# An expert stage on one core: the wait of v's rounding, and the place of the gathered rows' additions

## The chip, the cores and the metric

The kernel runs on one core of a Trainium2 chip. The metric is the device time of one execution in microseconds (us). All of the change lies in one of its stages, the one that computes the experts of a PEER layer (product-key retrieval). That stage takes about 2390 of 5121 us.

## The reference, cut to what matters

The whole program is one layer of an encoder: token mixers, cross-attention and then PEER. Of PEER, for 1152 tokens (1024 of a prompt, 128 of samples), this counts here:

```
idx = take_along_axis(cidx, top_k(cand, 16))        # 8 heads x 16 experts of 16384 per token
g = softmax(sc)
h = einsum('nd,nhkd->nhk', xb, u[idx])
a = gelu(h) * g
out = einsum('nhk,nhkd->nd', a, v[idx])
```

The earlier stages have found indices and gates. The expert stage computes h, a and out, and adds out to the residual H.

## The kernel before, in words

Tokens are nine tiles of 128 (NT = 9). The first three (NG = 3) are treated by gathering, the other six (ND = 6) densely. Both treatments share the steps e = 0 .. 127 of one loop (NKEY = 128).

*Dense tiles.* Step e takes the 128 experts of key e. TensorE computes `hidden`: h = u x for six tiles, in two halves c = 0 and 1 of 384 columns. Every fp32 operand is split in a rounded high half and a low half (fp32r), and a product takes three matmuls: high by high, low by high, high by low. That is 48 matmuls a step (L2077 to L2079). ScalarE takes the gelu out of PSUM (L1932, `gelu(c)`), VectorE multiplies by the gates w (L1993, `weigh(c)`), ScalarE rounds the product to its high half ah (L1936, `high_a(c)`), VectorE subtracts for the low half al (L2000, `low_a(c)`). TensorE's `output` multiplies ah and al by v for a group of two steps (GROUP = 2) and one half of the 1024 output columns, so there is one output per step, of 36 matmuls in six banks of PSUM (L2091 to L2093). VectorE adds each bank to H (L1983, `add_up`).

*Loads and their halves.* u, v and w of a step come by SP's queue. ScalarE rounds u and v (L1911 `high_u`, L1915 `high_v`), VectorE subtracts (L1974 `low_u`, L1978 `low_v`). The buffers of u, v, uh, ul, vh, vl and w are double. SP's order per step is: wait for ul, load u; wait for weigh(1), load w; wait for vl, load v. output(e) reads the halves of v written by high_v(e - 2), in buffer e % 2; high_v(e - 1) runs in step e and overwrites what output(e - 1) read.

*Gathered tiles.* Slot e of each of the 128 tokens of tile j names one expert. POOL gathers the 128 rows (u and v side by side, 2048 fp32 each, so 1 MB) with an indirect DMA (L1900) into uv[j], one buffer per j. VectorE's `dot(j)` multiplies with x and sums (L2004); ScalarE takes the gelu of the three results (L1941) and multiplies by the gates into three coefficients (L1945), behind a drain; VectorE's `add_row(j)` adds coefficient times v row to H (L2010). That frees uv[j] for the next gather.

*Order.* Each engine's order is written out by hand in its `step`. VectorE: drain, dot(0), low_u(e + 1), dot(1), low_v(e - 1), dot(2), weigh(0), low_a(0), weigh(1), add_row(0), low_a(1), then six add_ups with add_row(1) and add_row(2) between. ScalarE: high_u(e + 1), high_v(e - 1), gelu(0), high_a(0), gelu of the dots, gelu(1), drain, coefficients, high_a(1). TensorE: hidden(e), output(e). Steps 0 and 1 have no output and are written before the loop.

*The counters.* `y_ready` counts finished banks of output. output(out) starts at out = 2, so when output(out) ends it stands at NY * (out - 1), with NY = 6. Three places read it: ScalarE before high_v in a step (`NY * (e - 1)`), VectorE in add_up (`NY * (out - 2) + x + 1`), and ScalarE before the last high_v.

Of the kernel before, what the change touches and what calls it, by code (L numbers as in the profile page):

```python
# [1443 lines left out]
NKEY = 128  # L1444
# [356 lines left out]
NY = ND  # L1801


def phase_experts(nc, sem, K, I, S):


    with ExitStack() as ctx:
# [34 lines left out]
        y_ready = sem("ex_y_ready")  # L1842
# [6 lines left out]
        with nc.Block() as block:  # L1849
# [54 lines left out]
            @block.scalar  # L1904
            def _(act):
                act.sem_inc(h_taken, 2)
                act.sem_inc(ah_ready, 2)

                def high_u(e, s, turn):
                    act.wait_ge(u_in[s], 16 * (turn + 1))  # L1910
                    act.activation(uh[s][:, :, :], u[s][:, :, :], ACT.Copy).then_inc(uh_ready, 1)  # L1911

                def high_v(p, s, turn):
                    act.wait_ge(v_in[s], 16 * (turn + 1))
                    act.activation(vh[s][:, :, :], v[s][:, :, :], ACT.Copy).then_inc(vh_ready, 1)  # L1915

                def step(i, k, last=False):
                    e, s = i * 4 + k, k % 2
                    first = isinstance(i, int) and i == 0 and k < 2
                    if not last:  # L1920
                        if not first or k:
                            act.wait_ge(h_ready, 2 * e + 2)
                        high_u(e + 1, 1 - s, i * 2 + (k + 1) // 2)
                    if not first or k:
                        if not first:
                            act.wait_ge(y_ready, NY * (e - 1))
                        high_v(e - 1, 1 - s, i * 2 + (k - 1) // 2)

                    def gelu(c):
                        act.wait_ge(h_ready, 2 * e + c + 1 + 2)  # L1930
                        act.wait_ge(p_ready, 2 * e + c + 1)
                        act.activation(gel[:, c, :], hp[c][:, 0:TC], ACT.Gelu_apprx_tanh).then_inc(h_taken, 1)  # L1932

                    def high_a(c):
                        act.wait_ge(p_ready, 2 * e + c + 1 + 2)
                        act.activation(ah[k % 4][:, c * TC:(c + 1) * TC], prod[:, c, :], ACT.Copy).then_inc(ah_ready, 1)  # L1936

                    gelu(0)
                    high_a(0)
                    act.wait_ge(dotted, NG * (e + 1))  # L1940
                    act.activation(hg[s][:, :], hs[s][:, :], ACT.Gelu_apprx_tanh)  # L1941
                    gelu(1)
                    act.drain()
                    for j in range(NG):
                        done = act.activation(coef[s][:, j:j + 1], hg[s][:, j:j + 1], ACT.Copy,  # L1945
                                              scale=K["gate"][:, bass.ds(e, 1), j:j + 1].rearrange("p a n -> p (a n)"))
                    done.then_inc(weighed, 1)
                    high_a(1)

                high_u(0, 0, 0)  # L1950
                for t in range(ND):
                    act.wait_ge(x_in[t % 2], 16 * (t // 2 + 1))
                    act.activation(xh[:, :, t * P:(t + 1) * P],
                                   v[t % 2][:, :, :].rearrange("p a n -> p (a n)").rearrange("p (k n) -> p k n", k=KD),
                                   ACT.Copy).then_inc(xh_ready, 1)
                act.wait_ge(xl_ready, ND)
                step(0, 0)
                step(0, 1)
                with act.Fori(0, NKEY // 4 - 1) as i:
                    for k in range(2, 6):  # L1960
                        step(i, k)
                step(NKEY // 4 - 1, 2)
                step(NKEY // 4 - 1, 3, last=True)
                act.wait_ge(y_ready, NY * (NKEY - 1))
                high_v(NKEY - 1, 1, NKEY // 2 - 1)

            @block.vector
            def _(dve):
# [3 lines left out]
                def low_u(e, s):  # L1972
                    dve.wait_ge(uh_ready, e + 1)
                    dve.tensor_tensor(ul[s][:, :, :], u[s][:, :, :], uh[s][:, :, :], ALU.subtract).then_inc(ul_ready, 1)  # L1974

                def low_v(p, s):
                    dve.wait_ge(vh_ready, p + 1)
                    dve.tensor_tensor(vl[s][:, :, :], v[s][:, :, :], vh[s][:, :, :], ALU.subtract).then_inc(vl_ready, 1)  # L1978

                def add_up(out, half, x):  # L1980
                    dst = H[:, NG + x, half * CW:(half + 1) * CW]
                    dve.wait_ge(y_ready, NY * (out - 2) + x + 1)
                    dve.tensor_tensor(dst, dst, yp[x][:, :], ALU.add).then_inc(y_added, 1)  # L1983

                def step(i, k, last=False):
                    e, s = i * 4 + k, k % 2
                    first = isinstance(i, int) and i == 0 and k < 2

                    def weigh(c):
                        dve.wait_ge(h_taken, 2 * e + c + 1 + 2)  # L1990
                        dve.wait_ge(ah_ready, 2 * e + c + 1)
                        nb = TC // P
                        dve.tensor_tensor(prod[:, c, :].rearrange("p (b n) -> p b n", n=P),  # L1993
                                          gel[:, c, :].rearrange("p (b n) -> p b n", n=P),
                                          w[s][:, c * nb:(c + 1) * nb, :], ALU.mult).then_inc(p_ready, 1)

                    def low_a(c):
                        dve.wait_ge(ah_ready, 2 * e + c + 1 + 2)
                        at = slice(c * TC, (c + 1) * TC)
                        dve.tensor_tensor(al[k % 4][:, at], prod[:, c, :], ah[k % 4][:, at], ALU.subtract).then_inc(al_ready, 1)  # L2000

                    def dot(j):
                        dve.wait_ge(uv_in[j], 16 * (e + 1))
                        dve.scalar_tensor_tensor(out=uv[j][:, 0:D], in0=uv[j][:, 0:D], scalar=1.0, in1=gx[:, j, :],  # L2004
                                                 op0=ALU.mult, op1=ALU.mult, accum_out=hs[s][:, j:j + 1]).then_inc(dotted, 1)

                    def add_row(j):
                        if j == 0:
                            dve.wait_ge(weighed, e + 1)
                        dve.scalar_tensor_tensor(out=H[:, j, :], in0=uv[j][:, D:2 * D], scalar=coef[s][:, j:j + 1], in1=H[:, j, :],  # L2010
                                                 op0=ALU.mult, op1=ALU.add).then_inc(summed, 1)

                    dve.drain()
                    dot(0)
                    if not last:
                        low_u(e + 1, 1 - s)
                    dot(1)
                    if not first or k:
                        low_v(e - 1, 1 - s)
                    dot(2)  # L2020
                    dve.wait_ge(w_in[s], 16 * (i * 2 + k // 2 + 1))
                    weigh(0)
                    low_a(0)
                    weigh(1)
                    add_row(0)
                    low_a(1)
                    if first:
                        add_row(1)
                        add_row(2)
                        return  # L2030
                    add_up(e, s, 0)
                    add_up(e, s, 1)
                    add_row(1)
                    add_up(e, s, 2)
                    add_up(e, s, 3)
                    add_row(2)
                    add_up(e, s, 4)
                    add_up(e, s, 5)
# [7 lines left out]
                for t in range(ND):  # L2046
                    dve.wait_ge(xh_ready, t + 1)
                    dve.tensor_tensor(xl[:, :, t * P:(t + 1) * P],
                                      v[t % 2][:, :, :].rearrange("p a n -> p (a n)").rearrange("p (k n) -> p k n", k=KD),
                                      xh[:, :, t * P:(t + 1) * P], ALU.subtract).then_inc(xl_ready, 1)  # L2050
                step(0, 0)
                step(0, 1)
                with dve.Fori(0, NKEY // 4 - 1) as i:
                    for k in range(2, 6):
                        step(i, k)
# [8 lines left out]
            @block.tensor  # L2064
            def _(pe):
                pe.sem_inc(h_ready, 2)

                def hidden(i, k, first=False):
                    e, s = i * 4 + k, k % 2
# [247 lines left out]
```

## Time and profile before

| What | Value |
|---|---|
| Three runs, median (lowest to highest) | 5125.22 us (5123.2 to 5139.28) |
| The profiled execution | 5122.89 us, span 5121.1 us |
| TensorE matmuls busy | 4180.8 us, 82% |
| VectorE busy | 3170.4 us, 62% |
| ScalarE busy | 1286.5 us, 25% |
| GpSimd busy | 626.4 us, 12% |
| Expert stage | from about 2700 to 5090 us of the span |
| Granted TensorE clock | 0.89 mean over the span, 1.00 in the stage's steady part |

The profile is one execution. A row of the timeline gives start, duration, engine, line, operation, output and inputs, and in square brackets how long the engine idled before it and what released it. L1915 is line 1915 of the kernel. VectorE's and ScalarE's instructions overlap a little, so starts are subtracted, not durations added. "PEld" is TensorE's weight load. "Landing" of a DMA is the time from its launch until its data have arrived.

### The profile page before, as it was taken

The numbers are of one execution on the slowest core, as the hardware profiler recorded it, in microseconds if no ns is written. First come the engines' busy times: TensorE is split into PE (matmuls) and PEld (weight loads), VectorE is DVE, ScalarE is ACT, GpSimd is POOL, SyncE is SP. The second block draws the span as 40 slices with busy tenths as digits, with TensorE's granted clock in tenths as the row PEclk, the third lists the DMA queues.
The fourth block names the chain that finished last, engine by engine and source line by source line (L and its number), as shares of the span: only waits on it lengthen the run. The fifth ranks groups of instructions, "written<-read, shape, count | busy, mean of one in ns | idle before, by whom it ended". The sixth has DMA issues, their size and how long they took to land. (4 is left out here: it accounts for less than half of the span.)

```text
span 5121.1 us, 61600 instructions
## 1 busy us (share of the span) xinstructions
PE 4180.8 (82%) x20219; PEld 3460.1 (68%) x20219; DVE 3170.4 (62%) x5709; ACT 1286.5 (25%) x2699; POOL 626.4 (12%) x505
## 2 busy tenths in 40 slices
PE   6999898997878863455527999999999999999996
PEld 5787566784436753454426888888888888888885
DVE  4301332111112159999986888888888888888886
ACT  2111222111112111344532222222222222222222
POOL 0000000000000000344331111111111111111110
PEclk9999676558989876788878999999999999999998
DMA  3322311102121010111127667676767667776764
GB/s 133 111 95 80 94 31 37 36 0 98 33 90 66 0 38 9 70 70 70 70 123 258 250 250 248 251 250 250 250 248 252 250 249 250 249 252 250 249 250 163
DMA packets 308267, 770.86 MB, mean 151 GB/s; under 512 B 29120, under 2 KB 170944, under 8 KB 257728
## 3 DMA queue, kind: packets, MB, share of 16 engines
q0 software_dynamic: 55360, 403.60, 20.9%
q1 hardware_dynamic: 233376, 356.77, 20.5%
q10 hardware_dynamic: 19440, 9.44, 0.6%
q8 instruction: 37, 0.61, 0.0%
q14 instruction: 54, 0.44, 0.0%
HBM read 681.01 MB, written 89.78 MB: 151 GB/s over the span
## 5 line engine op out<-in xcount | busy, mean ns | idle before, releaser
L2077 PE MATMUL exp_h<-exp_xh,exp_uh 128*128 128x384 f32 x2048 | 701.4, 342 | 243.7 <-ACT exp_gel L1932 193.5
L2078 PE MATMUL exp_h<-exp_xl,exp_uh 128*128 128x384 f32 x2048 | 687.3, 336 | 0.0
L2079 PE MATMUL exp_h<-exp_xh,exp_ul 128*128 128x384 f32 x2048 | 686.9, 335 | 0.0
L1900 POOL DMA_INDIRECT exp_uv<-in_peer_uv,gidx x384 | 373.6, 973 | 2009.0 <-DVE H L2010 1971.0
L2091 PE MATMUL exp_y<-exp_vh,exp_ah 128*128 128x512 f32 x1536 | 598.8, 390 | 11.5 <-DVE H L1983 11.5
L2092 PE MATMUL exp_y<-exp_vl,exp_ah 128*128 128x512 f32 x1536 | 601.0, 391 | 0.0
L2093 PE MATMUL exp_y<-exp_vh,exp_al 128*128 128x512 f32 x1536 | 601.0, 391 | 0.0
L2077 PEld LDWEIGHTS exp_h<-exp_xh,exp_uh 128*128 128x128 f32 x2048 | 386.5, 189 | 297.5 <-ACT exp_gel L1932 242.6
L2004 DVE SCALAR_TENSOR_TENSOR exp_uv<-exp_uv,exp_gx 128x1024 f32<-128x1024 f32 x384 | 469.1, 1222 | 69.3 <-DMA exp_uv<-in_peer_uv,gidx 48.5
L2010 DVE SCALAR_TENSOR_TENSOR H<-exp_uv,exp_coef,H 128x1024 f32<-128x1024 f32 x384 | 492.1, 1282 | 23.8 <-ACT exp_coef L1945 23.8
L1983 DVE TENSOR_TENSOR H<-H,exp_y 128x512 f32<-128x512 f32 x768 | 491.2, 682 | 2.5 <-PE exp_y L2093 2.4
L1915 ACT ACTIVATE exp_vh<-exp_v 128x1024 fp32r<-128x1024 f32 x128 | 135.2, 1056 | 1179.9 <-PE exp_y L2093 1179.9
L2078 PEld LDWEIGHTS exp_h<-exp_xl,exp_uh 128*128 128x128 f32 x2048 | 386.9, 189 | 0.0
L2079 PEld LDWEIGHTS exp_h<-exp_xh,exp_ul 128*128 128x128 f32 x2048 | 386.6, 189 | 0.0
L2091 PEld LDWEIGHTS exp_y<-exp_vh,exp_ah 128*128 128x128 f32 x1536 | 289.1, 188 | 69.7 <-issue 8.7
L2093 PEld LDWEIGHTS exp_y<-exp_vh,exp_al 128*128 128x128 f32 x1536 | 288.9, 188 | 60.6
L2092 PEld LDWEIGHTS exp_y<-exp_vl,exp_ah 128*128 128x128 f32 x1536 | 288.9, 188 | 57.9
L1785 PE MATMUL top_k<-top_right,top_left 128*128 128x128 f32 x1536 | 208.0, 293 | 139.3 <-ACT top_tile_w L1596 89.5
L1556 POOL TENSOR_TENSOR top_right<-top_bare,top_gt 128x768 f32<-128x768 bf16 x96 | 233.6, 2438 | 621.4 <-DVE top_bare L1715 547.5
L1978 DVE TENSOR_TENSOR exp_vl<-exp_v,exp_vh 128x1024 fp32r<-128x1024 f32 x128 | 156.8, 1225 | 239.5 <-ACT exp_vh L1915 239.5
L1785 PEld LDWEIGHTS top_k<-top_right,top_left 128*128 128x128 f32 x1536 | 191.2, 203 | 157.4 <-ACT top_tile_w L1596 123.2
L363 PE MATMUL proj_z<-proj_wh,proj_xh 128*128 (+2 forms) x648 | 253.4, 391 | 3.9 <-DVE proj_wl L281 3.2
(276 smaller groups left out, 6390.0 us busy)
## 6 DMA issues: line engine op xcount, KB each, us to landing
exp_u<-in_peer_u SPq DMA_DIRECT2D x128, 512.0 KB, 4.8
exp_v<-in_peer_v SPq DMA_DIRECT2D x128, 512.0 KB, 4.0
exp_w<-s_w SPq DMA_DIRECT2D x128, 384.0 KB, 3.6
out_z<-proj_zs SPq DMA_DIRECT2D x72, 256.0 KB, 2.0
proj_w<-in_w_in SPq DMA_DIRECT2D x16, 1024.0 KB, 5.4
merge_gates<-out_z SPq DMA_DIRECT2D x9, 1024.0 KB, 5.0
s_zt<-proj_zt ACTq DMA_DIRECT2D x27, 256.0 KB, 2.3
exp_uv<-in_peer_uv,gidx POOLq DMA_INDIRECT x384, 5.5
```

Of the source, the lines that this page charges most:

```text
L363: pe.matmul(zp[t % 3][:, 0:width], xh[:, k, at], high, start=(k == 0), stop=False)
L1785: last = pe.matmul(kp[2 * r + n // 4][:, (n % 4) * P:(n % 4 + 1) * P], left[r][:, n, :], right[r][:, n, :], start=True, stop=True)
L1900: pool.indirect_dma_start(out=uv[j][:, :], out_offset=None, in_=I["peer_uv"], in_offset=bass.IndirectOffsetOnAxis(ap=K["gidx"][:, e, j:j + ...
L1983: dve.tensor_tensor(dst, dst, yp[x][:, :], ALU.add).then_inc(y_added, 1)
L2004: dve.scalar_tensor_tensor(out=uv[j][:, 0:D], in0=uv[j][:, 0:D], scalar=1.0, in1=gx[:, j, :], op0=ALU.mult, op1=ALU.mult, accum_out=hs[s][ ...
L2010: dve.scalar_tensor_tensor(out=H[:, j, :], in0=uv[j][:, D:2 * D], scalar=coef[s][:, j:j + 1], in1=H[:, j, :], op0=ALU.mult, op1=ALU.add).t ...
L2077: pe.matmul(hp[c][:, 0:TC], uh[s][:, n, :], xh[:, n, at], start=(n == 0), stop=False)
L2078: pe.matmul(hp[c][:, 0:TC], uh[s][:, n, :], xl[:, n, at], start=False, stop=False)
L2079: last = pe.matmul(hp[c][:, 0:TC], ul[s][:, n, :], xh[:, n, at], start=False, stop=(n == KD - 1))
L2091: pe.matmul(yp[x][:, :], ah[a + n][:, rows], vh[half][:, n, :], start=(n == 0), stop=False)
L2092: pe.matmul(yp[x][:, :], ah[a + n][:, rows], vl[half][:, n, :], start=False, stop=False)
L2093: last = pe.matmul(yp[x][:, :], al[a + n][:, rows], vh[half][:, n, :], start=False, stop=(n == GROUP - 1))
```

## The change

Three edits. TensorE raises `y_ready` by NY once at the start, and the readers' thresholds are set anew: add_up's and the last high_v's by the same NY more, the one of high_v in a step left as it was. ScalarE's order in a step becomes gelu(0), high_a(0), gelu(1), high_a(1), and then the wait for the dots, their gelu, the drain and the coefficients. VectorE's becomes weigh(0), low_a(0), weigh(1), low_a(1), add_up 0, add_row(0), add_up 1, add_row(1), and on as before.

```
                     gelu(0)
                     high_a(0)
+                    gelu(1)
+                    high_a(1)
                     act.wait_ge(dotted, NG * (e + 1))
                     act.activation(hg[s][:, :], hs[s][:, :], ACT.Gelu_apprx_tanh)
-                    gelu(1)
                     act.drain()
                     for j in range(NG):
                         done = act.activation(coef[s][:, j:j + 1], ...)
                     done.then_inc(weighed, 1)
-                    high_a(1)
...
-                act.wait_ge(y_ready, NY * (NKEY - 1))
+                act.wait_ge(y_ready, NY * NKEY)
                 high_v(NKEY - 1, 1, NKEY // 2 - 1)
...
                 def add_up(out, half, x):
-                    dve.wait_ge(y_ready, NY * (out - 2) + x + 1)
+                    dve.wait_ge(y_ready, NY * (out - 1) + x + 1)
...
                     weigh(1)
-                    add_row(0)
                     low_a(1)
                     if first:
+                        add_row(0)
                         add_row(1)
                         add_row(2)
                         return
                     add_up(e, s, 0)
+                    add_row(0)
                     add_up(e, s, 1)
                     add_row(1)
...
                 pe.sem_inc(h_ready, 2)
+                pe.sem_inc(y_ready, NY)
```

## Rows read from the trace of the kernel before

**Rows 1.** Waits by line, 3000 to 5000 us (total, times, longest).

```profile
ACT exp_vh L1915 <- PE exp_y L2093: 1007.6, 109, 9.9
PEld exp_h L2077 <- ACT exp_gel L1932: 214.6, 109, 2.0
DVE exp_vl L1978 <- ACT exp_vh L1915: 200.4, 105, 2.2
...
DVE exp_uv L2004 <- DMA exp_uv<-in_peer_uv,gidx: 35.4, 42, 2.4
```

**Rows 2.** Timeline of TensorE: two first matmuls of hidden, 55 steps apart.

```profile
3993.38 0.45 PE L2077 MATMUL exp_h<-exp_xh,exp_uh 128*128 128x384 f32 x1 [1.52 <-ACT exp_gel L1932]
...
5002.19 0.45 PE L2077 MATMUL exp_h<-exp_xh,exp_uh 128*128 128x384 f32 x1 [1.52 <-ACT exp_gel L1932]
```

**Rows 3.** Timeline of VectorE, one step from low_v to low_v.

```profile
3992.98 1.22 DVE L1978 TENSOR_TENSOR exp_vl<-exp_v,exp_vh 128x1024 fp32r<-128x1024 f32 x1 [2.15 <-ACT exp_vh L1915]
...
3995.27 0.55 DVE L1993 TENSOR_TENSOR exp_prod<-exp_gel,exp_w 128x384 f32<-128x384 f32 x1
3996.41 0.56 DVE L2000 TENSOR_TENSOR exp_al<-exp_prod,exp_ah 128x384 fp32r<-128x384 f32 x1 [0.59 <-ACT exp_ah L1936]
3996.97 0.56 DVE L1993 TENSOR_TENSOR exp_prod<-exp_gel,exp_w 128x384 f32<-128x384 f32 x1
3997.71 1.29 DVE L2010 SCALAR_TENSOR_TENSOR H<-exp_uv,exp_coef,H 128x1024 f32<-128x1024 f32 x1 [0.18 <-ACT exp_coef L1945]
3998.92 0.56 DVE L2000 TENSOR_TENSOR exp_al<-exp_prod,exp_ah 128x384 fp32r<-128x384 f32 x1
3999.38 1.28 DVE L1983 TENSOR_TENSOR H<-H,exp_y 128x512 f32<-128x512 f32 x2
...
4002.97 1.28 DVE L2010 SCALAR_TENSOR_TENSOR H<-exp_uv,exp_coef,H 128x1024 f32<-128x1024 f32 x1
...
4005.65 1.23 DVE L2004 SCALAR_TENSOR_TENSOR exp_uv<-exp_uv,exp_gx 128x1024 f32<-128x1024 f32 x1 [0.20 <-issue]
...
4011.39 1.23 DVE L1978 TENSOR_TENSOR exp_vl<-exp_v,exp_vh 128x1024 fp32r<-128x1024 f32 x1 [2.22 <-ACT exp_vh L1915]
```

**Rows 4.** Timeline of ScalarE in the same step.

```profile
3995.86 0.53 ACT L1936 ACTIVATE exp_ah<-exp_prod 128x384 fp32r<-128x384 f32 x1 [2.53 <-DVE exp_prod L1993]
3996.29 0.19 ACT L1941 ACTIVATE exp_hg<-exp_hs 128x3 f32<-128x3 f32 x1
...
3997.01 0.66 ACT L1945 ACTIVATE exp_coef<-exp_hg,gate 128x1 f32<-128x1 f32 x3 [0.16 <-issue]
...
3999.94 1.06 ACT L1911 ACTIVATE exp_uh<-exp_u 128x1024 fp32r<-128x1024 f32 x1 [1.85 <-DMA exp_u<-in_peer_u]
```

**Rows 5.** Timeline of GpSimd: launches of the second and third gather.

```profile
4002.13 0.94 POOL L1900 DMA_INDIRECT exp_uv<-in_peer_uv,gidx  x1 [1.38 <-DVE H L2010]
4004.52 0.94 POOL L1900 DMA_INDIRECT exp_uv<-in_peer_uv,gidx  x1 [1.45 <-DVE H L2010]
```

**Rows 6.** Landing of gathers (L1900): 3000 to 5000 us; that of 4004.52.

```profile
DMA to landing us min/median/max: 5.2/5.5/8.3
...
DMA to landing us min/median/max: 5.6/5.6/5.6
```

**Rows 7.** Timeline of VectorE, a step with a slow first gather.

```profile
4933.16 1.28 DVE L2010 SCALAR_TENSOR_TENSOR H<-exp_uv,exp_coef,H 128x1024 f32<-128x1024 f32 x1 [0.18 <-ACT exp_coef L1945]
...
4942.31 1.23 DVE L2004 SCALAR_TENSOR_TENSOR exp_uv<-exp_uv,exp_gx 128x1024 f32<-128x1024 f32 x1 [1.42 <-DMA exp_uv<-in_peer_uv,gidx]
```

**Rows 8.** Timeline of VectorE, the three dots of step 1.

```profile
2741.69 1.22 DVE L2004 SCALAR_TENSOR_TENSOR exp_uv<-exp_uv,exp_gx 128x1024 f32<-128x1024 f32 x1 [2.82 <-DMA exp_uv<-in_peer_uv,gidx]
...
2744.60 1.22 DVE L2004 SCALAR_TENSOR_TENSOR exp_uv<-exp_uv,exp_gx 128x1024 f32<-128x1024 f32 x1 [0.54 <-DMA exp_uv<-in_peer_uv,gidx]
...
2747.50 1.23 DVE L2004 SCALAR_TENSOR_TENSOR exp_uv<-exp_uv,exp_gx 128x1024 f32<-128x1024 f32 x1 [0.53 <-DMA exp_uv<-in_peer_uv,gidx]
```

**Rows 9.** Windows: busy us of PE, PEld, DVE, ACT, POOL, clock, DMA share, GB/s.

```profile
3000.00:3200.00 200.00, 183.05 (x918) 163.61 (x917) 167.96 (x234) 50.34 (x110) 31.68 (x33) 1.00 0.70 249
```

More of the change, by code:

```diff
@@ L1939, in step @@
                     high_a(0)
+                    gelu(1)
+                    high_a(1)
                     act.wait_ge(dotted, NG * (e + 1))
                     act.activation(hg[s][:, :], hs[s][:, :], ACT.Gelu_apprx_tanh)
-                    gelu(1)
                     act.drain()
@@ L1947, in step @@
                     done.then_inc(weighed, 1)
-                    high_a(1)
                 high_u(0, 0, 0)
@@ L1963, in _ @@
                 step(NKEY // 4 - 1, 3, last=True)
-                act.wait_ge(y_ready, NY * (NKEY - 1))
+                act.wait_ge(y_ready, NY * NKEY)
                 high_v(NKEY - 1, 1, NKEY // 2 - 1)
@@ L1981, in add_up @@
                     dst = H[:, NG + x, half * CW:(half + 1) * CW]
-                    dve.wait_ge(y_ready, NY * (out - 2) + x + 1)
+                    dve.wait_ge(y_ready, NY * (out - 1) + x + 1)
                     dve.tensor_tensor(dst, dst, yp[x][:, :], ALU.add).then_inc(y_added, 1)
@@ L2024, in step @@
                     weigh(1)
-                    add_row(0)
                     low_a(1)
                     if first:
+                        add_row(0)
                         add_row(1)
@@ L2031, in step @@
                     add_up(e, s, 0)
+                    add_row(0)
                     add_up(e, s, 1)
@@ L2066, in _ @@
                 pe.sem_inc(h_ready, 2)
+                pe.sem_inc(y_ready, NY)
                 def hidden(i, k, first=False):
```

## The prediction

> **What bounds the kernel now.** I first read the busy share in 40 slices: the second half is one uniform stage, TensorE at nine tenths, VectorE at eight. That is the expert stage. The page's chain of waits says nothing here (every entry is 0%), so I took the waits grouped by line in 2000 us of that stage [rows 1]. They close a ring. ScalarE's rounding of v (L1915) waits 1007.6 us for the last output matmul; TensorE's next first matmul waits 214.6 us for the gelu (L1932) that stands behind that rounding; VectorE's low half of v waits 200.4 us for the rounding. There are 109 steps in it, so 1.97, and 1.84 us, per step. The period is (5002.19 - 3993.38)/55 = 18.34 us [rows 2]. TensorE alone would need 18.34 - 1.97 = about 16.4.
>
> Why the ring closes: in step e ScalarE waits at L1915 for `NY * (e - 1)`, which is output(e) finished, although the buffer it overwrites was last read by output(e - 1). gelu(0) of hidden(e) sits behind it, and hidden(e + 1) needs that gelu. So hidden(e + 1) can't start before output(e) has ended plus a rounding (0.97 from start to the next start) plus a gelu.
>
> **The change, part by part.** *The wait.* TensorE's one increment of `y_ready` by NY at the start makes `NY * (e - 1)` mean output(e - 1). VectorE's threshold in add_up rises by the same NY, and so does the wait before the last high_v: these mean what they did, cost 0, and the serial tail stays. ScalarE now runs high_u, high_v, gelu(0) in a row as soon as the u rows are in: 3999.94 + 1.06 + 1.0 + 0.5, so about 4002.5 [rows 4]. VectorE asks for the low half of v only at 4011.39 - 2.22 = 4009.2 [rows 3], so its wait (2.22 us in the step shown) goes, with 6 us to spare, and hidden(e + 1) no longer waits for gelu(0), with 7 us to spare. What is late next is VectorE.
>
> *VectorE's own cadence.* From low half of v to low half of v one step took 4011.39 - 3992.98 = 18.41, less the wait 2.22: 16.19 us [rows 3]. This holds 0.59 of waiting for ah (row 3996.41), 0.18 for the coefficients (row 3997.71) and 0.20 behind the drain (row 4005.65). add_row(0) used to stand between weigh(1) and low_a(1) and hid high_a(1). Now low_a(1) meets its ah directly: the same pair of engines as in weigh(0), low_a(0), so the same 0.59 again. The 0.18 goes if the coefficients are ready: high_a(1) starts 0.59 after weigh(1) starts, hg 0.43 later (3996.29 - 3995.86 [rows 4]), it lasts 0.19, drain 0.16, three coefficients 0.66: ready at weigh(1) + 2.03. add_row(0) now starts at weigh(1) + 1.14 + 0.46 + 0.60 (low_a's start, low_a, one add_up) = 2.20. Covered by 0.17; without that cover it costs up to the 0.18 of today. Sum: 16.19 + 0.59 - 0.18 = 16.60 us. That is above TensorE's 16.4, so TensorE gets slack and VectorE sets the pace: of the 1.97 us only some 1.7 can come out.
>
> *ScalarE's new order.* gelu(1) now stands behind high_a(0), not behind the wait for the dots and hg: its start is hg's old place, 0.09 earlier. It ends at weigh(0) + 1.49, and weigh(1) starts at weigh(0) + 1.70. TensorE's second half (c = 1) of hidden(e + 1) needs gelu(1), so it may start at weigh(0) + 1.6. From there to the next such point TensorE has 16.4 us of work, and VectorE's weigh(0) comes 16.6 or more later: TensorE will show a short idle time in the middle of hidden, and that costs nothing as long as VectorE is the slower. add_up finds its output finished several us earlier. No DMA issue of SP moves past another; load_v and load_u still follow VectorE's low_v, load_w follows weigh(1).
>
> *The gathers.* add_row(j) frees uv[j]; POOL launches the next gather, dot(j) of the next step reads it. Launch is 1.55 after add_row's start (4004.52 - 4002.97 [rows 3, 5]), landing 5.5 after that in the median (5.2 to 8.3 [rows 6]): 7.05 us from add_row's start to data. Room for the first gather before: 4005.65 - 3997.71 = 7.94. The edit puts add_row(0) behind low_a(1) and one add_up, 0.46 + 0.60 closer to dot(0): 6.88 us. A wait of 0.17 appears in every ordinary step where there was none. A slow gather shows what the rest costs: add_row(0) at 4933.16, dot(0) at 4942.31, 9.15 apart [rows 7]; it waited 1.42, and would wait 2.27. In the stage's DVE rows 23 of 108 first dots waited for their gather (42 of all 329 dots [rows 1]); I take one step in five as slow. Before, such waits were absorbed, since VectorE waited for v anyway. Now they are paid.
>
> The third gather is tighter than it looks. Its room was 7.34 plus the 2.22 of waiting (add_row(2) at 4002.97, next low_v at 4011.39, dot(2) 1.14 behind it, half of the 2.29 from low_v to weigh(0)), so it falls to 7.34. And the gathers come closer together: add_row(0) to add_row(1) was 2.87 (low_a 1.21 behind it, two add_ups 0.46 behind that, 1.20 for the two), now 1.20 + 0.60 = 1.80; the third still follows by 2.39. How fast can gathers follow one another? Below: launched 2.39 behind the second [rows 5], the third landed after 5.6, 0.1 over the median [rows 6], which is 2.5 at most if that 0.1 is queueing, and less if it isn't. Above: in the first steps, launched by three add_rows in a row, the three dots were released at 2741.69, 2744.60 and 2747.50, 2.90 apart [rows 8], with the stage's first loads beside them. With 2.5, the second is 0.7 late and the third 0.8: 7.05 + 0.8 - 7.34 = 0.5 of waiting. With no queueing it is the 0.17 of the first gather; with 2.9, 1.1 + 0.5 late, 1.3. Waits of one step do not add, the largest counts. I take 0.55, near the row without other loads, because in the new order the w load (issued behind weigh(1)) has landed before the gathers flow.
>
> The Trainium skill bears on this in two places of "DMA: Bandwidth & Descriptors". Its section Anatomy of one DMA gives 2.0 us plus bytes over 436 GB/s; for 128 rows of 8 KB that is an estimated 2.4 us of flow, which would leave the 0.17 to 0.3 of waiting and a time near 4990. Its Specifications put a core's HBM limit near 358 GB/s: an estimate of 2.9 us a gather, 1.3 of waiting and a time near 5090. The landings in [rows 6] agree with the first, the arrivals in [rows 8] with the second.
>
> *Sum.* Mean wait 0.8 x 0.55 + 0.2 x 2.27 = 0.89. Period 16.60 + 0.89 = 17.49, 0.85 less than 18.34, over 125 periods (steps 2 to 127): 106 us. The profiled execution took 5122.9 (span 5121.1): 5017. The three timed runs have their median 2.3 above it, which I leave out. Bounds: no queueing and slow gathers in one step of ten, 0.38, gives 16.98 and 4953; 2.9 us a gather, with slow steps at 3.0, gives 1.64, 18.24 and 5110.
>
> **Rivals.** *A, the gathers stay hidden.* If they land faster in the new spacing (nothing flows beside them), only the 16.60 of VectorE remains: 1.74 x 125 = 217, so 4905. For it: 0.17 is small and the shortest landing is 5.2. Against: the slow fifth.
>
> *B, the gathers become the bound on every step (slower).* Three closer gathers, and u, v and w in a shorter period, push all landings to the slow steps' 7.6 (9.15 - 1.55): 16.60 + 2.27 = 18.87, 0.53 more than now, 66 us: 5189. It decides from a first landing of 1.74 + 6.88 - 1.55 = 7.07 us on, where 16.60 plus the wait reaches 18.34. For it: maxima of 8.3 exist at today's load, and [rows 8] show a queue. Against: the median is at the bottom of its range.
>
> *C, the change doesn't free the ring.* ScalarE's high_v would find v not in, or gelu(1), now tied to weigh(0), would hold TensorE in the place of gelu(0), each giving back what was won: 5123. Against: v's buffer is reloaded right behind the low half before and read two steps later, and TensorE's idle time in the middle of hidden (above) does not reach VectorE, whose add_ups read an output that ended several us before.
>
> **How the numbers follow.** Forecast 0.74 (5017; its own range 4953 to 5085), A 0.12, B 0.07, C 0.07. About 0.3% (15 us) is what a measurement can tell from no change. Faster: forecast and A, less 0.01 for the upper bound: 0.85. Within: C and that 0.01, 0.08. Slower: 0.07. The range runs from 4900, to take in A, to 5085; outside are B, C and the forecast's top, 0.18.
>
> **What would show it.** The wait of L1915 on exp_y and of L1978 on exp_vh gone; low_a (L2000) waiting 0.59 twice a step, twice the 0.59 of before; L2010 waiting near nothing for the coefficients; L2004 waiting for the gathers about 0.9 us a step, in nearly every step, most of it before dot(0) and dot(2); TensorE idle about 1 us a step, now in the middle of hidden. The granted clock (1.00 in the stage [rows 9], its 2.4 GHz level, through 1.97 us of idling per step) stays there. Wrong would be: a wait at L1978 that stays, a sum of L2004's waits under 0.3 (A) or over 1.7 us a step (B), or landings well away from 5.5 to 6.4.

## The result: 5151.28 us, and the profile after

The median of 20 runs is 5151.28 us (5132.0 to 5168.27), beside 5126.45 us (5113.84 to 5141.1) for the kernel before. The ratio is 1.0037, with a 95% interval of 1.0025 to 1.0049: 0.4% slower and clear of no change, where 5017 was forecast. The profiled execution took 5133.94 us (span 5132.2), near the fastest of the 20 and 17 us under their median. In it the steps 2 to 127 last 20.7 us longer than in the profile before (their first dots stand at 2734.6 and 5068.6, before at 2741.7 and 5055.1); the stage began 9.4 us earlier, so that the whole execution shows only 11 us.

First the waits by line, 3000 to 5000 us (line, who for whom, total us, times, longest). They answer to [rows 1].

```profile
ACT exp_ah L1936 <- DVE exp_prod L1993: 1419.0, 218, 13.7
DVE exp_uv L2004 <- DMA exp_uv<-in_peer_uv,gidx: 217.3, 244, 2.2
PEld exp_h L2079 <- ACT exp_gel L1932: 186.2, 106, 2.7
...
DVE exp_al L2000 <- ACT exp_ah L1936: 128.6, 218, 0.6
```

(L2079 is L2077 of before, L2010 and L2004 keep their numbers.) The ring is gone: no row of L1915 waits for exp_y and none of L1978 for exp_vh. In its place VectorE waits for the gathers in nearly every step, 217.3 us where [rows 1] had 35.4. Over 85 of these steps the waits before dot(0), dot(1) and dot(2) average 0.58, 1.28 and 0.15 us, 2.01 in all, of which 0.20 is the drain. The mean period is 18.47 us. TensorE's wait of 186.2 us, 1.7 a step, stands for the most part in the middle of hidden: the second half waits for gelu(1), which stands behind high_a(0), and that one waits for VectorE's weigh(0).

GpSimd's launches of one step, and VectorE's dots that follow (start, duration, then the idle time before and who ended it):

```profile
4022.70 0.94 POOL L1900 DMA_INDIRECT exp_uv<-in_peer_uv,gidx  x1 [13.77 <-DVE H L2010]
4024.49 0.94 POOL L1900 DMA_INDIRECT exp_uv<-in_peer_uv,gidx  x1 [0.86 <-DVE H L2010]
4026.88 0.94 POOL L1900 DMA_INDIRECT exp_uv<-in_peer_uv,gidx  x1 [1.46 <-DVE H L2010]
```

```profile
4021.15 1.28 DVE L2010 SCALAR_TENSOR_TENSOR H<-exp_uv,exp_coef,H 128x1024 f32<-128x1024 f32 x1
...
4022.94 1.28 DVE L2010 SCALAR_TENSOR_TENSOR H<-exp_uv,exp_coef,H 128x1024 f32<-128x1024 f32 x1
...
4028.26 1.23 DVE L2004 SCALAR_TENSOR_TENSOR exp_uv<-exp_uv,exp_gx 128x1024 f32<-128x1024 f32 x1 [0.46 <-DMA exp_uv<-in_peer_uv,gidx]
...
4031.61 1.22 DVE L2004 SCALAR_TENSOR_TENSOR exp_uv<-exp_uv,exp_gx 128x1024 f32<-128x1024 f32 x1 [0.97 <-DMA exp_uv<-in_peer_uv,gidx]
```

The landings of those three launches, and then of all gathers from 3000 to 5000 us (min, median, max), against [rows 6]:

```profile
DMA to landing us min/median/max: 5.5/5.5/5.5
...
DMA to landing us min/median/max: 7.1/7.1/7.1
...
DMA to landing us min/median/max: 7.4/7.4/7.4
...
DMA to landing us min/median/max: 5.4/7.4/8.7
```

The first gather lands as before. The second is launched 1.79 us behind it and takes 7.1; from add_row(1) at 4022.94 to dot(1) at 4031.61 pass 8.67 us, where VectorE's own work between the two, with the drain, takes 7.36 and the rest is waiting, before dot(0) and before dot(1).

### The profile page after: what moved, and what is told of

It is laid out like the page before. It is cut to its first block and busy times, and to the rows that moved or that the text cites. A ratio compares the mean times of both kernels' runs of the same rounds, so it can differ in the third digit from the quotient of the medians.

```text
span 5132.2 us, 61601 instructions
## 1 busy us (share of the span) xinstructions
PE 4204.5 (82%) x20219; PEld 3491.5 (68%) x20219; DVE 3166.6 (62%) x5709; ACT 1285.1 (25%) x2699; POOL 621.1 (12%) x505
## 5 line engine op out<-in xcount | busy, mean ns | idle before, releaser
L2079 PE MATMUL exp_h<-exp_xh,exp_uh 128*128 128x384 f32 x2048 | 715.0, 349 | 232.4 <-ACT exp_gel L1932 177.2
L2081 PE MATMUL exp_h<-exp_xh,exp_ul 128*128 128x384 f32 x2048 | 700.7, 342 | 0.0
L2080 PE MATMUL exp_h<-exp_xl,exp_uh 128*128 128x384 f32 x2048 | 700.2, 342 | 0.0
L2004 DVE SCALAR_TENSOR_TENSOR exp_uv<-exp_uv,exp_gx 128x1024 f32<-128x1024 f32 x384 | 470.3, 1225 | 275.2 <-DMA exp_uv<-in_peer_uv,gidx 265.1
L1900 POOL DMA_INDIRECT exp_uv<-in_peer_uv,gidx x384 | 368.9, 961 | 2035.3 <-DVE H L2010 1995.1
L2079 PEld LDWEIGHTS exp_h<-exp_xh,exp_uh 128*128 128x128 f32 x2048 | 395.3, 193 | 278.6 <-ACT exp_gel L1932 216.0
L1936 ACT ACTIVATE exp_ah<-exp_prod 128x384 fp32r<-128x384 f32 x256 | 134.1, 524 | 1661.5 <-DVE exp_prod L1993 1661.5
L2010 DVE SCALAR_TENSOR_TENSOR H<-exp_uv,exp_coef,H 128x1024 f32<-128x1024 f32 x384 | 490.0, 1277 | 0.6 <-ACT exp_coef L1946 0.6
L364 PE MATMUL proj_z<-proj_wl,proj_xh 128*128 (+2 forms) x648 | 249.6, 385 | 0.0
```

Of the source, the lines that this page charges most:

```text
L1900: pool.indirect_dma_start(out=uv[j][:, :], out_offset=None, in_=I["peer_uv"], in_offset=bass.IndirectOffsetOnAxis(ap=K["gidx"][:, e, j:j + ...
L2079: pe.matmul(hp[c][:, 0:TC], uh[s][:, n, :], xh[:, n, at], start=(n == 0), stop=False)
L2080: pe.matmul(hp[c][:, 0:TC], uh[s][:, n, :], xl[:, n, at], start=False, stop=False)
L2081: last = pe.matmul(hp[c][:, 0:TC], ul[s][:, n, :], xh[:, n, at], start=False, stop=(n == KD - 1))
```

## The experiments

The two theories after the result were S (spacing: a gather launched 1.8 us behind another lands some 2 us later, one launched 2.3 us or more behind doesn't) and L (load: landings grow with the transfers per time). "Landings" below are those of 3000 to 5000 us. The passages in frames are what was expected of each run. "The changed kernel" is the one of the result; "ratio" is to the kernel before, run beside.

**The wait alone** (wait_only). The kernel before with the three edits of `y_ready`, and no other.

```
                 pe.sem_inc(h_ready, 2)
+                pe.sem_inc(y_ready, NY)
...
-                    dve.wait_ge(y_ready, NY * (out - 2) + x + 1)
+                    dve.wait_ge(y_ready, NY * (out - 1) + x + 1)
...
-                act.wait_ge(y_ready, NY * (NKEY - 1))
+                act.wait_ge(y_ready, NY * NKEY)
```

> The corrected wait alone, with VectorE's and ScalarE's order of before. Theory S (spacing): a gather launched 1.8 us behind another lands about 2 us later (7.4 instead of 5.4), launched 2.3 us or more behind it doesn't. Here the launches are again 2.9 and 2.4 apart, so landings go back to a median of 5.5, VectorE's step is 16.2 us plus some 0.6 of waiting for gathers, the period 16.8, the time about 4935 (4900 to 4980). Theory L (load): landings grow because a shorter period puts more transfers into the same time; then the median stays near 7.4, each step waits 1.5 to 1.8 us for gathers, and the time is 5050 to 5130.

Measured: 4933.45 us (4925.15 to 4938.99), ratio 0.9611 (0.9589 to 0.9632). S gave 4935. The waits and the landings, 3000 to 5000 us:

```profile
ACT exp_ah L1936 <- DVE exp_prod L1993: 1209.7, 112, 13.8
...
DVE exp_uv L2004 <- DMA exp_uv<-in_peer_uv,gidx: 68.1, 94, 2.0
...
PEld exp_h L2078 <- ACT exp_gel L1932: 24.9, 29, 1.7
```

```profile
DMA to landing us min/median/max: 5.3/5.7/8.3
```

With a mean period of 16.76 us, more transfers per time than in the changed kernel's 18.47, the median landing is 5.7. That is against L. The correction is worth 193.6 us by itself (5127.04 beside it), and the new order on top of it costs 218 (5151.28 - 4933.45), more than all of that.

**The order alone** (order_only). The changed kernel with `y_ready` as before.

```
-                pe.sem_inc(y_ready, NY)
...
-                    dve.wait_ge(y_ready, NY * (out - 1) + x + 1)
+                    dve.wait_ge(y_ready, NY * (out - 2) + x + 1)
...
-                act.wait_ge(y_ready, NY * NKEY)
+                act.wait_ge(y_ready, NY * (NKEY - 1))
```

> The new order of VectorE and ScalarE alone, with the over-tight wait of before. S: launches are 1.8 and 2.4 apart, so the landing's median is 7.4 although the period cannot be shorter than before's 18.3 us; VectorE's 1.7 us of slack takes most of the waiting, the time is 5120 to 5190. L: at the old period the landings stay at 5.5, the time is that of before.

Measured: 5149.02 us (5135.61 to 5163.67), ratio 1.0032 (1.0016 to 1.0049), which is the changed kernel's time. Its waits:

```profile
ACT exp_vh L1915 <- PE exp_y L2094: 971.7, 108, 9.8
...
DVE exp_uv L2004 <- DMA exp_uv<-in_peer_uv,gidx: 214.0, 245, 2.3
```

The landings are the changed kernel's (median 7.4) with the old ring still there (L1915 waits as before), so they come from the order. And with that order the corrected wait changes nothing: the mean period is 18.5 us with the old ring and without it.

**More room for descriptors** (scratch_12k). One cause of S could be that the second gather's descriptors find no room in the memory that the kernel sets aside for them (`dynamic_dma_scratch_size`).

```
-    nc = _bacc.Bacc("TRN2", ..., dynamic_dma_scratch_size=4096)
+    nc = _bacc.Bacc("TRN2", ..., dynamic_dma_scratch_size=12288)
```

> The changed kernel with 12288 instead of 4096 bytes a partition for the gathers' descriptors. If the late second gather waits for room for its descriptors (theory D, one cause of S), its landing falls to 5.5 to 6.5 and the time to 4960 to 5020. If not, landings (median 7.4) and time (5150) stay.

Measured: 5142.05 us (5135.71 to 5151.43), ratio 1.0028 (1.0016 to 1.0039); landings 5.4/7.4/8.7 as in the changed kernel. That cause is out, as far as three times the room can tell.

**add_row(1) and add_row(2) one add_up later each** (rows_spaced), so that launches are 2.4 and 2.4 apart.

```
                     add_up(e, s, 1)
-                    add_row(1)
                     add_up(e, s, 2)
+                    add_row(1)
                     add_up(e, s, 3)
-                    add_row(2)
                     add_up(e, s, 4)
+                    add_row(2)
```

> The changed kernel with add_row(1) and add_row(2) one add_up later each, so that the launches are 2.4 and 2.4 apart. S: landings go back to 5.5; the rooms from add_row to dot are then 6.9, 6.8 and 6.7 us against 7.05 needed, waiting 0.3 us in ordinary steps and 0.7 in the mean, the period 17.3, the time 4980 to 5015, although each gather has less room than in the changed kernel. L: landings stay at 7.4 and the lost room makes it slower than the changed kernel, 5180 to 5230.

Measured: 5056.56 us (5051.81 to 5060.91), ratio 0.9859 (0.9837 to 0.9880). The direction is S's, and L, which gave 5180 to 5230, is refuted: less room, and yet 95 us faster than the changed kernel. The landings' median is 5.7. The size was missed by 40 us or more: third gathers average 6.4 us, not 5.5, and the waits 1.34 us a step with the drain, not 0.7; the period is 17.8, not 17.3.

**Launches held back, first try** (launch_held). VectorE's and ScalarE's order as in the changed kernel; GpSimd waits for the add_up behind the add_row too.

```
                             pool.wait_ge(summed, NG * (e - 1) + j + 1)
+                        if e > 2 and j:
+                            pool.wait_ge(y_added, NY * (e - 2) + 2 * j + 1)
```

> The changed kernel, its orders untouched, but GpSimd launches the second and third gather only when VectorE has also finished the add_up behind the add_row, 0.6 us later. S: launches are 2.4 apart, the second lands after 5.7 to 6.0 in place of 7.5, so its data arrive 1.0 us or more earlier although it starts 0.6 later; the time falls to 5040 to 5090, near that of rows_spaced. If the distance of the launches is not the cause, the landings stay at 7.4 and the kernel is slower than the changed one by 0.6 us a step, about 5225.

Measured: 5274.12 us (5269.15 to 5280.8), ratio 1.0285 (1.0248 to 1.0322): 184 us above S's range, and 49 above the 5225 of the other theory. By itself it would speak against S. The trace shows that it did not try S cleanly:

```profile
4029.19 0.94 POOL L1902 DMA_INDIRECT exp_uv<-in_peer_uv,gidx  x1 [12.23 <-DVE H L2012]
4032.09 1.83 POOL L1902 DMA_INDIRECT exp_uv<-in_peer_uv,gidx  x1 [1.96 <-DVE H L1985]
4034.48 0.94 POOL L1902 DMA_INDIRECT exp_uv<-in_peer_uv,gidx  x1 [0.56 <-DVE H L1985]
```

The second launch came 2.90 us behind the first, not 2.4, and took 1.83 us, not 0.94; it landed after 6.4, which is 9.3 us behind the first launch. The third came 2.39 us behind the start, but only 0.56 behind the end, of that long launch, and landed after 7.5. Both gathers start later behind the first than was meant.

**Launches held back by one wait** (one_wait_held). The same with the second wait in place of the first: VectorE ends the add_row before it ends the add_up.

```
-                        if e:
+                        if e > 2 and j:
+                            pool.wait_ge(y_added, NY * (e - 2) + 2 * j + 1)
+                        elif e:
                             pool.wait_ge(summed, NG * (e - 1) + j + 1)
```

> launch_held again without its side cost: its GpSimd had two waits ahead of a launch, launched 0.8 us behind the second of them, and the launch itself took 1.83 us in place of 0.94. Here there is one wait, for the add_up behind the add_row (VectorE ends the add_row before it). S: the launches are 2.4 and 2.4 apart, the second gather lands after 5.7 to 6.1 in place of 7.5, its data arrive 0.8 to 1.2 us sooner although it starts 0.6 us later, and the time is 5030 to 5090. If the distance is not the cause: landings 7.4, time about 5225.

Measured: 5052.14 us (5037.15 to 5071.23), ratio 0.9870 (0.9835 to 0.9905). One step's launches, and the landing of the second:

```profile
4023.92 0.94 POOL L1902 DMA_INDIRECT exp_uv<-in_peer_uv,gidx  x1 [11.23 <-DVE H L2012]
4026.31 0.94 POOL L1902 DMA_INDIRECT exp_uv<-in_peer_uv,gidx  x1 [1.45 <-DVE H L1985]
4028.70 0.94 POOL L1902 DMA_INDIRECT exp_uv<-in_peer_uv,gidx  x1 [1.45 <-DVE H L1985]
```

```profile
DMA to landing us min/median/max: 5.6/5.6/5.6
```

VectorE, ScalarE and TensorE work in the order of the changed kernel here, and the second and the third launch start 0.6 us later; the second's data arrive 8.0 us behind the first launch (2.39 + 5.6) instead of 8.9 (1.79 + 7.1), and the kernel gains 99 us. This shows the spacing as the cause.

The DMA packets in the traces of these two kernels show what the spacing changes. A gather is 128 packets of 8 KB, most of which take 0.31 us. In the mean of all steps from 3000 to 5000 us, with the packets in order of their start and times from the first launch (the split between two gathers is good to a few packets):

```
                                                       changed kernel   one_wait_held
launch of the second gather                                     1.83            2.40
last packet of the first gather starts                          4.82            4.80
first packet of the second gather starts                        4.84            4.84
packets of the second gather that take over 0.6 us              10.5             1.5
last packet of the second gather starts                         7.82            7.39
second gather landed                                            9.31            8.38
```

So there is a queue: the second gather's packets follow the first's at once, at the same time in both kernels, and the earlier launch gains nothing. What comes on top, 0.93 us, arises after the first of its packets has started: in the changed kernel the packets take longer, and the landing comes later still behind the start of the last (1.49 in place of 0.99). Other transfers are not the reason: between 1.5 and 8 us behind the first launch the loads of u, v and w move less than 1 KB a step in either kernel.

**Half the bytes** (half_rows). The gather takes only the v half of a row, and dot and add_row both work on it; the u half is left out, so this kernel serves for its time alone.

```
-  pool.indirect_dma_start(out=uv[j][:, :], out_offset=None, in_=I["peer_uv"],
+  pool.indirect_dma_start(out=uv[j][:, 0:D], out_offset=None, in_=I["peer_v"].rearrange("a b d -> (a b) d"),
...
-  dve.scalar_tensor_tensor(out=H[:, j, :], in0=uv[j][:, D:2 * D], scalar=coef[s][:, j:j + 1], in1=H[:, j, :],
+  dve.scalar_tensor_tensor(out=H[:, j, :], in0=uv[j][:, 0:D], scalar=coef[s][:, j:j + 1], in1=H[:, j, :],
```

> The changed kernel with half the bytes per gathered row: it leaves out the u half of the rows, and dot and add_row both use the v half. Launches stay 1.8 apart. If the second gather is late because two gathers' data share the 16 DMA engines (theory B, bytes), 0.5 MB flow in half the time: the second lands after 4.5 to 5.5, close to the first, nothing waits but TensorE's own 16.4 us, and the time is 4890 to 4930. If it is a cost per gather or per row whatever its size (theory G), the second still lands 1.5 to 2 us later than the first, 6.0 to 6.5; VectorE then waits little (room 7.36 against 7.6 to 8.0), and the time is 4930 to 4980.

Measured: 4891.96 us (4877.56 to 4894.51), ratio 0.9531 (0.9494 to 0.9568). The first gather lands after 4.29 us in the mean, the second after 5.06. Lateness fell from 1.84 (7.48 - 5.64) to 0.77 with the bytes. That is nearer B (bytes) than G, whose 6.0 to 6.5 is not seen; but half the bytes still leave a lateness, at the same 1.8 us, so a part per gather isn't excluded.

**The load of w later** (w_late). wait_only, and SP loads w behind v.

```
                     sp.wait_ge(p_ready, 2 * (e + 1) + 2)
-                    load_w(e + 2, s)
                     sp.wait_ge(vl_ready, e + 1)
                     load_v(i + 1, s)
+                    load_w(e + 2, s)
```

> wait_only with the load of w issued behind that of v instead of behind weigh(1), so that it no longer flows just before the first gather. In wait_only one first gather in ten lands after 7.7, and 31 of 88 third dots wait; in the changed kernel, where the first gather comes 1 us later behind the w load, hardly any first gather is slow (90% within 5.9). If the w load is what makes them slow (theory W), 90% of first landings come within 6.0 and the time falls by 30 to 60 us to 4875 to 4905. If the slow ones come by themselves, landings and time stay: 4933.

Measured: 4890.92 us (4881.36 to 4900.66), ratio 0.9538 (0.95 to 0.9576), as W had it: 90% of first gathers land within 5.8 us (within 7.5 in wait_only).

**Dots later** (dots_late). wait_only, with the two lows of u and v first and dot(2) behind weigh(0), and ScalarE's gelu(1) earlier (conditions and waits are left out of the cut).

```
                     dve.drain()
-                    dot(0)
                     low_u(e + 1, 1 - s)
-                    dot(1)
                     low_v(e - 1, 1 - s)
-                    dot(2)
+                    dot(0)
+                    dot(1)
                     weigh(0)
+                    dot(2)
                     low_a(0)
...
                     high_a(0)
+                    gelu(1)
                     act.wait_ge(dotted, NG * (e + 1))
                     act.activation(hg[s][:, :], hs[s][:, :], ACT.Gelu_apprx_tanh)
-                    gelu(1)
```

> wait_only with VectorE's order low_u, low_v, dot(0), dot(1), weigh(0), dot(2), low_a(0), weigh(1) and so on, and ScalarE's gelu(1) ahead of its wait for the dots. Launches stay 2.9 and 2.4 apart, each gather has 0.6 to 2.3 us more room, and dot(2) fills the 0.59 us in which VectorE waited for ah. VectorE's step is then 15.6 us and TensorE's 16.4 the bound: period 16.45, 4890 (4880 to 4915). If TensorE was the bound of wait_only already, no gain: 4933.

Measured: 4891.48 us (4876.41 to 4905.77), ratio 0.9548 (0.9504 to 0.9592). Its first gathers are quick too (90% within 5.8), with w where it was. So it isn't w by itself: here weigh(1), and with it the w load and the first launch, come some 1.7 us later behind the loads of v and u. That a first gather is slow when launched while the three loads still flow is argued from these two, not tried apart.

**Both** (both_late). dots_late with w_late's edit.

> dots_late with w_late's order of the loads. Each alone came to 4891 with TensorE never waiting in the stage; if TensorE's 16.4 us a step are the bound, the two together give the same, 4880 to 4895; only if the 0.1 us a step that dots_late still lay above w_late was VectorE's or ScalarE's does it gain 10 us.

Measured: 4886.24 us (4873.76 to 4894.12), ratio 0.9529 (0.9501 to 0.9557). It can't be told from either alone. One window of 1800 us (columns as in [rows 9]), first of wait_only, then of both:

```profile
3000.00:4800.00 1800.00, 1784.44 (x9017) 1620.26 (x9016) 1633.51 (x2255) 479.32 (x1073) 311.05 (x324) 1.00 0.78 274
```

```profile
3000.00:4800.00 1800.00, 1800.00 (x9138) 1642.50 (x9137) 1635.84 (x2286) 523.72 (x1089) 313.93 (x326) 1.00 0.78 277
```

TensorE is never idle any more: it is the bound of this stage (w_late and dots_late show 1800.00 too), and w_late, dots_late and both are all 4.5 to 4.7% faster than before.

## Why the prediction was wrong, step by step

*Right.* The ring and its mechanism: wait_only shows that opening it is worth 194 us. The waits at L1915 and L1978 gone. VectorE's own cadence, forecast 16.60: measured 18.47 - 2.01 + 0.20 = 16.66. The second 0.59 at low_a (128.6 us in 218 waits). The coefficients ready in time (add_row no longer waits for them). TensorE idle in the middle of hidden, at no cost. The sign of each edit's effect on the gathers' room.

*Off in size.* The first gather's wait, forecast 0.17 in an ordinary step: 0.38 in the mean (0.58 less the drain's 0.20). TensorE's idle time, forecast about 1 us a step: 1.7. The granted clock was to stay at 1.00: it was 0.97 to 1.00.

*The step that failed* is the term "mean wait 0.8 x 0.55 + 0.2 x 2.27 = 0.89". It measured 1.81 (2.01 less the drain's 0.20), so the period was 18.47 in place of 17.49, and a gain of 106 us became a loss. Inside it, the sentence "the second is 0.7 late and the third 0.8" is what broke. Measured, the second is 1.84 late (7.48 - 5.64) and the third 2.08 (7.72 - 5.64). With these landings the prediction's own rooms give 7.72 + 1.55 - 7.34 = 1.93 of waiting for the third gather, near the 1.81: the rooms were right, the landings were not. It took launches 1.8 us apart as a queue, in which a later start never means an earlier arrival. The queue is there, and explains about half: 2.4 us behind the first the second is 0.38 late (one_wait_held, 5.98 - 5.60), and starting 0.57 sooner adds 0.57. The other 0.93 is no queueing: launching 0.6 us later made the data arrive 0.93 sooner. So in the changed kernel the second arrives 3.67 us after the first (9.31 - 5.64), above both of the bounds taken for it, 2.5 and 2.9.

The trace of before could have told. In five steps, every 26th, its third gather was launched 1.85 us behind the second, because the second was launched late (2.39 us of idling before it, where 1.85 is usual). Timeline and landing of the third in one of them:

```profile
3360.80 0.94 POOL L1900 DMA_INDIRECT exp_uv<-in_peer_uv,gidx  x1 [2.39 <-DVE H L2010]
3362.65 0.94 POOL L1900 DMA_INDIRECT exp_uv<-in_peer_uv,gidx  x1 [0.91 <-DVE H L2010]
```

```profile
DMA to landing us min/median/max: 7.4/7.4/7.4
```

Those five landed after 6.9 to 7.5. Among other slow gathers they don't stand out; sorted by the distance to the launch before, they are the row for the new spacing. And [rows 8], three gathers launched 1.7 and 2.0 us apart, were taken as the upper bound with 2.9 us a gather: the second dot of that step was 2.91 behind the first because its gather landed after 6.6, the first's after 5.4.

*The rivals.* B named the right loop and its price of a wait (1.74 us to break even; 1.87, that is 18.47 - 16.60, came), at a chance of 0.07. Its cause was only in part the right one: not all landings rose, the first stayed at 5.64, well under the 7.07 from which B was to decide, and the load per time did not matter (wait_only). In ordinary steps the slow fifth of first gathers vanished, which B and the forecast both had wrong. A did not happen: the waits of L2004 were 2.01 us a step, not under 0.3. Whether it would have held with the old spacing was not tried; no run has the new order of add_row(0) with launches 2.9 us apart. C did not happen either, though the outcome lay near its 5123: that is luck of the number. Of the sentences on "DMA: Bandwidth & Descriptors" in the Trainium skill, the one on its Specifications (an estimate of 2.9 us a gather) came nearer in time than the one on its section Anatomy of one DMA (2.4); neither holds a jump by spacing. Where the prediction says that the landings in [rows 6] agree with the Anatomy section, that holds for the estimate of 2.4 us of flow alone (the packets show 8 on each DMA engine of 0.31 us, 2.5 us); the section's whole sum, an estimate of 4.4 us for a gather, does not agree with the 5.5 of [rows 6].

## What to carry to other kernels

Two edits that each looked small did not add: the wait gained 194 us alone and nothing beside the reorder, because the reorder built a second loop (buffer freed, gather, dot) as long as the ring that was removed. Before moving what frees a single buffer, write down the room from the freeing to the next use and the distance between launches, and look in the trace of before for the few instances that already have the new distance. Sort latencies by that distance rather than taking a median and a tail.

## What the runs showed of the hardware

Landing of a 1 MB gather by the distance to the launch before it, 3000 to 5000 us of before, the changed kernel, wait_only, order_only, scratch_12k, rows_spaced, w_late and dots_late, where the one before landed in under 5.8 us (min, median, max in us; three more gathers, at 1.4 and 3.0, are left out):

```
distance     count   landing
1.8 to 1.9     313     6.2  7.5  8.6
2.3             27     5.5  5.9  7.5
2.4            482     5.3  5.7  7.4
2.9            352     5.2  5.5  6.5
3.4             15     5.2  5.5  6.2
```

Between 1.85 and 2.31 us of distance, where these runs have no launch, the median landing falls by 1.6. Behind a gather that is itself late 2.4 us don't suffice: in the changed kernel the third, launched 2.4 behind the late second, lands after 7.7. What makes the second gather's packets slower at 1.8 us stays open: not the room for descriptors (scratch_12k), not the other loads (none flow then), partly the bytes (half_rows: 4.29 and 5.06).

With two waits ahead of its launch every second gather of launch_held started 0.5 us later and lasted 1.83 instead of 0.94 us (against one_wait_held); the third gathers, with two waits as well, lasted 0.94. The long launch isn't tied to two waits: in 2000 us of the changed kernel five first launches, with one wait each, lasted 1.8 as well. And TensorE's granted clock, 1.00 in this stage before, was 0.97 to 1.00 in the 200 us windows of the changed kernel, where TensorE stopped in the middle of hidden; it was 1.00 in wait_only and in order_only. No cost of it shows: order_only, with the clock at 1.00 throughout the stage, has the same ratio to before (1.0032 against 1.0037).
